# Memory's root applied to the products, wide chunks for the keys' weights, and another order of the first loads

## The chip, the cores and the metric

One Trainium2 chip, one of its cores. The metric is the device time of one launch, in microseconds. Engines are named as in the profile: PE is TensorE (PEld its weight loads), DVE is VectorE, ACT is ScalarE, POOL is GpSimd, SP is SyncE, which here only issues DMAs.

## The reference, cut to what matters

The whole reference is three transformer-like layers on a sequence of 256 tokens of width 2048, with a memory of 256 tokens. What the change touches is how memory's keys and values come about, for the second and the third layer:

```python
def rms_norm_2(x, w):
    xf = x.astype(jnp.float32)
    y = xf * lax.rsqrt(jnp.mean(xf * xf, axis=-1, keepdims=True) + EPS)
    return (y * w.astype(jnp.float32)).astype(x.dtype)

mem_n = rms_norm_2(mem, mem_norm_w)                 # 256 x 2048
k = (mem_n @ w_mk).reshape(b_, -1, MEM_HEADS, MEM_HEAD_DIM)   # 2048 x 512, once per layer
v = (mem_n @ w_mv).reshape(b_, -1, MEM_HEADS, MEM_HEAD_DIM)   # 2048 x 512, once per layer
```

The first layer's input is modulated: silu(c) times w_ada (2048 x 6144) gives shift, scale and gate, and h = rms_norm(x) * (1 + scale) + shift, which is multiplied with w_in.

## The kernel before, in words

Activations are kept transposed: 16 tiles of 128 features by 256 tokens. Every large product is a `Gemm` (line 88), cut into blocks of output columns and chunks of 0.5 MB of weights. For each chunk SP loads the raw weights into one of 7 slots (line 391), ACT writes a rounded high part (`split_hi`, line 410), DVE the remainder as low part (`split_lo`, line 416), and TensorE multiplies (`run_products`, line 457): high weights with the high and low halves of x side by side (line 484, 512 columns), low weights with the high half of x (line 485, 256 columns). For values, kept by token, x is the stationary side and each tile takes six matmuls of 512 columns (lines 478 to 480). A chunk's slot is loaded again once the chunk is used; ACT and DVE split 3 chunks ahead (AHEAD). PSUM holds two sets of two banks for the products (SETS, `set_of`), and a block may start once the block two before it has been taken out.

The order of the work is that of `ORDER` (line 341), the same on all engines. First stand the four products on memory, `G_MEM` (line 291): keys of the second layer (8 chunks of 4 tiles x 256 columns, two blocks side by side), values (8 chunks of 2 tiles x 512 columns), keys and values of the third layer: 32 chunks, called units 0 to 31 here. Behind them come the products on xA, the first layer's normed input.

All other work is hung between the chunks by hooks, written out by hand as positions (i, p) or units. In the memory stage these are: the sum of squares of x on ACT (`norm_square`, line 626), on GpSimd (`add_squares`, line 572, three of four groups are added in pairs) and on TensorE (`sum_squares`, line 1801, matmuls with a matrix of ones from the constants con; line 1810), ending in a root on ACT (`norm_inverse_root`, line 647); and the sums of silu(c) w_ada on DVE (`ada_add`, line 1213), 32 steps in units 0 to 27. GpSimd issues the loads of w_ada (line 588) into a ring of 6 buffers: load m may be issued when the step 6 before it is done. At unit 28 TensorE turns the sums into columns (`modulation_columns`, line 1829), and in units 29 to 31 ACT and DVE norm the first half of x.

Every engine works its queue in order, so a wait holds all that stands behind it. Before the first product on memory the whole of memory's norm is done: SP loads vec, the four quarters of memory, con, then weights (lines 549 to 559); ACT squares the quarters (line 730) and splits three chunks; GpSimd adds; TensorE sums (line 1839); ACT makes the root; DVE multiplies each tile by gain and root (line 1115), ACT writes the high part to xM (line 660), DVE the low part (line 1122). GpSimd issues its first load of w_ada after its adds. Products of keys are taken out by ACT's copy of one half (line 453) and DVE's add of the other (line 1177), values by one copy (line 451).

## Time and profile before

| what | us |
|---|---|
| median of 3 runs | 1816.09 (1813.1 to 1817.1) |
| the profiled execution | 1821.62 |
| its span | 1819.8 |
| TensorE busy in the span | 1767.1 |

The span is what the profiler records on the core; the profiled execution's own time lies 1.8 us above it. All times inside the trace count from the span's start. A busy TensorE is not TensorE at its peak, since ends of matmuls are modelled; where its granted clock is 0.50 each matmul takes twice as long at the same busy share.

### The profile page before, as it was taken

What the parts mean: (1) busy time and instruction counts of PE and PEld (TensorE: products, weight loads), DVE (VectorE), ACT (ScalarE), POOL (GpSimd) and SP (SyncE); (2) the same over time, 40 slices, a digit from 0 to 9 for tenths busy, and PEclk for the clock granted to TensorE, in tenths of its full rate; (3) what the DMA queues carried; (4) which work ended last, traced back from release to release, by engine and by line L of the source; (5) the groups of instructions that cost most, each with busy time, mean ns of one, the idle gap of its engine ahead of it and who ended that gap; (6) DMA issues with size and microseconds to landing.
All of it is one profiled execution on the core that took longest, in us unless ns stands there. A gap on an engine that the chain in (4) does not pass through costs nothing.

```text
span 1819.8 us, 24336 instructions
## 1 busy us (share of the span) xinstructions
PE 1767.1 (97%) x9667; PEld 1501.8 (83%) x9667; DVE 1289.3 (71%) x1631; ACT 897.1 (49%) x1158; POOL 120.0 (7%) x147
## 2 busy tenths in 40 slices
PE   5899999999999999999999999899999999999997
PEld 4688888777888888888888888788888888888886
DVE  6888978785677756888676777965555667677654
ACT  4444443344465445665344556644444445565532
POOL 2411101010010100111000000000000000000000
PEclk9999999999999999999999999999999999999999
DMA  9989969674445566666654555555566565444563
GB/s 319 358 309 336 337 219 322 222 242 134 146 145 171 185 175 187 193 182 179 165 146 141 152 161 171 164 188 184 187 183 173 169 192 149 124 120 127 162 185 105
DMA packets 311889, 350.70 MB, mean 193 GB/s; under 512 B 11248, under 2 KB 286832, under 8 KB 311776
## 3 DMA queue, kind: packets, MB, share of 16 engines
q1 hardware_dynamic: 297792, 298.34, 54.3%
q0 software_dynamic: 13984, 50.80, 7.9%
q8 instruction: 78, 1.28, 0.3%
q14 instruction: 35, 0.29, 0.1%
HBM read 347.00 MB, written 2.10 MB: 192 GB/s over the span
## 4 chain that ended last, share of the span: by engine, by line
PE 78%; DVE 12%; ACT 4%; issue 3%; DMA 2%; POOL 0%; SPq 0%; ACTq 0%; DVEq 0%
PE psG L484 42%; PE psG L485 21%; DVE w_lo L418 4%; PE psG L478 2%; PE psG L479 2%; PE psG L480 2%; ACT w_hi L414 2%; PE psH L1810 1%; DMA raw<-in_mem_w 1%; PE psH L1799 1%; DMA ada_ring<-in_w_ada 1%; DVE P L1177 1%; PE psH L1824 1%; DVE P L1182 1%; PE psH L2108 1%
## 5 line engine op out<-in xcount | busy, mean ns | idle before, releaser
L484 PE MATMUL psG<-xA,w_hi 128*128 128x512 f32 x2624 | 947.0, 404 | 3.4 <-DVE w_lo L418 3.4
L418 DVE TENSOR_TENSOR w_lo<-raw,w_hi 128x1024 fp32r<-128x1024 f32 (+1 forms) x560 | 688.9, 1241 | 262.0 <-ACT w_hi L414 260.6
L485 PE MATMUL psG<-xA,w_lo 128*128 128x256 f32 x2624 | 737.4, 281 | 0.0
L414 ACT ACTIVATE w_hi<-raw 128x1024 fp32r<-128x1024 f32 (+1 forms) x560 | 569.4, 1043 | 233.1 <-PE psG L485 166.3
L484 PEld LDWEIGHTS psG<-xA,w_hi 128*128 128x128 f32 x2624 | 494.6, 188 | 129.0 <-issue 14.9
L485 PEld LDWEIGHTS psG<-xA,w_lo 128*128 128x128 f32 x2624 | 497.7, 190 | 4.1 <-issue 3.6
L484 PE MATMUL psG<-yP,w_hi 128*128 128x512 f32 x960 | 340.0, 398 | 3.1 <-DVE P L1182 1.6
L485 PE MATMUL psG<-yP,w_lo 128*128 128x256 f32 x960 | 269.2, 280 | 0.0
L484 PEld LDWEIGHTS psG<-yP,w_hi 128*128 128x128 f32 x960 | 180.2, 188 | 47.4 <-DVE P L1182 1.9
L453 ACT ACTIVATE P<-psG 128x512 f32<-128x512 f32 (+2 forms) x103 | 61.0, 592 | 247.4 <-PE psG L485 247.4
L485 PEld LDWEIGHTS psG<-yP,w_lo 128*128 128x128 f32 x960 | 181.3, 189 | 0.2
L1177 DVE TENSOR_TENSOR P<-psG,P 128x512 f32<-128x512 f32 (+2 forms) x103 | 70.4, 683 | 115.7 <-ACT P L453 115.7
L1224 DVE SCALAR_TENSOR_TENSOR ada_sum<-ada_ring,silc,ada_sum 128x1024 f32<-128x1024 f32 x60 | 77.9, 1302 | 0.1
L588 POOL DMA_DIRECT2D ada_ring<-in_w_ada x96 | 50.8, 530 | 329.8 <-DVE ada_sum L1224 133.2
L577 POOL TENSOR_TENSOR W<-W 128x512 f32<-128x512 f32 x15 | 25.8, 1720 | 664.3 <-ACT W L632 664.3
L1197 DVE TENSOR_TENSOR xT<-psG,xT 128x512 f32<-128x512 f32 x32 | 22.1, 692 | 54.5 <-PE psG L485 53.9
L484 PE MATMUL psG<-xM,w_hi 128*128 128x512 f32 x128 | 47.6, 413 | 5.3 <-DVE xM L1122 4.8
L478 PE MATMUL psG<-w_hi,xA 128*128 128x512 f32 x128 | 52.7, 411 | 0.0
L484 PE MATMUL psG<-xQ,w_hi 128*128 128x512 f32 x144 | 51.1, 399 | 0.0
L479 PE MATMUL psG<-w_lo,xA 128*128 128x512 f32 x128 | 51.0, 399 | 0.0
L480 PE MATMUL psG<-w_hi,xA 128*128 128x512 f32 x128 | 50.9, 398 | 0.0
L485 PE MATMUL psG<-xQ,w_lo 128*128 128x256 f32 x144 | 40.4, 281 | 0.0
(311 smaller groups left out, 1768.1 us busy)
## 6 DMA issues: line engine op xcount, KB each, us to landing
raw<-in_w_in SPq DMA_DIRECT2D x360, 512.0 KB, 3.8
raw<-in_w_out SPq DMA_DIRECT2D x128, 512.0 KB, 3.5
ada_ring<-in_w_ada POOLq DMA_DIRECT2D x96, 512.0 KB, 6.1
raw<-in_mem_w SPq DMA_DIRECT2D x32, 512.0 KB, 8.8
raw<-in_w_uq SPq DMA_DIRECT2D x24, 384.0 KB, 3.3
raw<-in_w_ukv SPq DMA_DIRECT2D x32, 128.0 KB, 2.4
raw<-in_w_ukv SPq DMA_DIRECT2D x16, 256.0 KB, 3.4
P<-in_memT SPq DMA_DIRECT2D x4, 512.0 KB, 5.8
```

The source lines that it names most:

```text
L414: nc.scalar.activation(high(n), low(n, raw), ACT.Copy).then_inc(hi_ready, 1)
L418: nc.vector.tensor_tensor(low(n), low(n, raw), high(n), ALU.subtract).then_inc(lo_ready, 1)
L453: nc.scalar.activation(g.dst(b), product(g, b, 0), ACT.Copy).then_inc(copied, 1)
L478: nc.tensor.matmul(out, x_hi, hi[:, w], start=first, stop=False)
L479: nc.tensor.matmul(out, x_hi, lo[:, w], start=False, stop=False)
L480: last = nc.tensor.matmul(out, x_lo, hi[:, w], start=False, stop=end)
L484: nc.tensor.matmul(psG[:, bank + f, :], hi[:, w], x, start=first, stop=False)
L485: last = nc.tensor.matmul(psG[:, bank + f, S:2 * S], lo[:, w], x[:, 0:S], start=False, stop=end)
L577: nc.gpsimd.tensor_tensor(a[:, 0:512], a[:, 0:512], a[:, 512:1024], ALU.add).then_inc(q["nm_pair"], 1)
L588: pool.dma_start(ada_ring[slot][:, :], ada_rows(k, part, half)).then_inc(ada_loaded[slot], 16)
L1177: ins = v.tensor_tensor(out, product(g, b, 1), out, ALU.add)
L1224: v.scalar_tensor_tensor(out=out, in0=src, scalar=silc[:, k:k + 1], in1=out, op0=ALU.mult, op1=ALU.add).then_inc(ada_used, 1)
```

## The change

Memory's products are now made on memory times the norm's weights (gain), without the root. The root of each token is applied when the products are taken out: for keys DVE multiplies the block with the root, laid out along tokens, in tile 80 of P (as products of the later layers already do); for values, where tokens are partitions, ACT scales its copies by a column, which TensorE makes from the root by two matmuls of one column. The high parts of memory's tiles are written by ACT from the raw tiles and the low parts by DVE, four tiles at a time: the first four before the products, the others in units 0, 2 and 4. The squares of memory move from before the products into ACT's units 0, 1, 3 and 5, its sums into TensorE's units 3 to 6, its root into unit 7; the squares and sums of x move to units 8 to 14 and 10 to 16.

The keys' weights come as 2 tiles x 512 columns, as the values' do: 8 chunks for both blocks together, which use all four banks and end together. SP's first loads are vec, memory 0, weights 0 and 1, memory 1, weights 2 and 3, memory 2, weights 4, memory 3, weights 5 and 6, con, weights 7, x. GpSimd waits for memory's second quarter and then issues its loads of w_ada; memory's adds stand before its loads 6, 7 and 9, those of x before loads 12, 14 and 17. DVE's w_ada steps lie in units 4 to 28, two in units 4, 8, 12, 16, 20, 24 and 28 and one in the others.

```diff
@@ -99,17 +100,18 @@
...
     def __init__(self, kt, blocks, src, x, dst=None, cols=256, kk=4, ready=None, tokens=None, pair=False, rows=NP,
-                 bias=None, by_tile=False, adds=False, per=None, norm=None):
+                 bias=None, by_tile=False, adds=False, per=None, norm=None, wide=False):
         self.kt, self.blocks, self.src, self.x, self.dst, self.cols, self.kk = kt, blocks, src, x, dst, cols, kk
...
         self.copied, self.by_scalar = not adds and bool(dst), not adds and bool(tokens)
-        self.chunks, self.parts = kt // kk, cols // NP
-        self.order = [(b, c) for b in range(blocks) for c in range(self.chunks)]
+        self.chunks, self.parts, self.wide = kt // kk, cols // NP, wide
+        self.order = [(b, c) for b in range(1 if wide else blocks) for c in range(self.chunks)]
         if pair:
             self.order[0:2 * self.chunks] = [(b, c) for c in range(self.chunks) for b in range(2)]
-        self.last = [self.order.index((b, self.chunks - 1)) for b in range(blocks)]
+        self.last = [self.chunks - 1 if wide else self.order.index((b, self.chunks - 1)) for b in range(blocks)]
+        self.elements = kk * cols * (blocks if wide else 1)
         self.c0 = self.b0 = self.landed0 = self.copied0 = 0
@@ -289,11 +292,16 @@
...
         G_MEM = []
+        def whole_rows(i):
+            return lambda block, chunk: rows(mem_w, (i * KT + 2 * chunk) * NP, 2, 0, 512)
         for i in range(2):
-            at0 = dict(x=lambda k: xM[:, k, :], ready=norm_ready(0))
-            G_MEM += [Gemm(KT, 2, columns(mem_w, 0, row0=2 * i * KT * NP), dst=lambda b, i=i: memkv[:, 8 * i + 2 * b:8 * i + 2 * b + 2, :],
-                           pair=i == 0, **at0),
-                      Gemm(KT, 1, columns(mem_w, 0, 512, 2, row0=(2 * i + 1) * KT * NP), cols=512, kk=2,
+            at0 = dict(x=lambda k: xM[:, k, :], ready=norm_ready(0), kk=2, norm=0)
+            G_MEM += [Gemm(KT, 2, whole_rows(2 * i), dst=lambda b, i=i: memkv[:, 8 * i + 2 * b:8 * i + 2 * b + 2, :],
+                           wide=True, **at0),
+                      Gemm(KT, 1, whole_rows(2 * i + 1), cols=512,
                            tokens=by_head(memkv[:, 8 * i + 4:8 * i + 8, :]), **at0)]
@@ -382,13 +390,13 @@
...
             g = CHUNKS[n][0]
-            return w_hi[:, n % HIGH_SLOTS, 0:g.kk * g.cols]
+            return w_hi[:, n % HIGH_SLOTS, 0:g.elements]
...
             g = CHUNKS[n][0]
-            return (w_lo if t is None else t)[:, PLACE["weight", n] % SLOTS, 0:g.kk * g.cols]
-        def load_weights(sp, g):
+            return (w_lo if t is None else t)[:, PLACE["weight", n] % SLOTS, 0:g.elements]
+        def load_weights(sp, g, behind=None):
             j = PLACE["weight", g.c0]
@@ -402,6 +410,8 @@
...
                     sp.dma_start(out, src).then_inc(raw_loaded[j % SLOTS], 16)
+                if behind:
+                    behind(c)
@@ -428,8 +438,9 @@
...
                 hook(s, p + 1)
-                if i == g.last[b]:
-                    block_done(b)
+                for block in range(g.blocks):
+                    if i == g.last[block]:
+                        block_done(block)
@@ -448,8 +459,12 @@
...
                     src = src.rearrange("p h (t d) -> p h t d", t=4)
+                if g.norm is not None:
+                    nc.scalar.activation(out[:, 0], src[:, 0], ACT.Copy, scale=mem_root_col[:, 0:1])
+                    nc.scalar.activation(out[:, 1], src[:, 1], ACT.Copy, scale=mem_root_col[:, 1:2]).then_inc(scalar_landed, 1)
+                    return
                 nc.scalar.activation(out, src, ACT.Copy).then_inc(scalar_landed, 1)
-            elif g.bias is None or g.norm:
+            elif g.bias is None or g.norm is not None:
                 nc.scalar.activation(g.dst(b), product(g, b, 0), ACT.Copy).then_inc(copied, 1)
@@ -458,9 +473,10 @@
...
                 n, bank = g.c0 + i, set_of(g, b)
-                if c == 0 and g.b0 + b >= SETS:
-                    before, block = BLOCKS[g.b0 + b - SETS]
-                    landed(pe, before, block + 1)
+                for a in range(2 if g.wide else 1):
+                    if c == 0 and g.b0 + b + a >= SETS:
+                        before, block = BLOCKS[g.b0 + b + a - SETS]
+                        landed(pe, before, block + 1)
                 if g.ready:
@@ -479,10 +495,12 @@
...
                     else:
-                        for f in range(g.parts):
-                            w = slice(kk * g.cols + f * NP, kk * g.cols + f * NP + NP)
-                            nc.tensor.matmul(psG[:, bank + f, :], hi[:, w], x, start=first, stop=False)
-                            last = nc.tensor.matmul(psG[:, bank + f, S:2 * S], lo[:, w], x[:, 0:S], start=False, stop=end)
+                        width = g.elements // g.kk
+                        for f in range(width // NP):
+                            w = slice(kk * width + f * NP, kk * width + f * NP + NP)
+                            to = set_of(g, b + f // g.parts) + f % g.parts
+                            nc.tensor.matmul(psG[:, to, :], hi[:, w], x, start=first, stop=False)
+                            last = nc.tensor.matmul(psG[:, to, S:2 * S], lo[:, w], x[:, 0:S], start=False, stop=end)
                     if kk == g.kk - 1:
@@ -513,7 +531,7 @@
...
-            return C("dup", S) if n == 2 else W[:, 1536:1536 + S] if n == 3 else W[:, 0:S]
+            return (P[:, MEM_ROOT, :], W[:, 0:S], C("dup", S), W[:, 1536:1536 + S], W[:, 0:S])[n]
@@ -549,12 +567,21 @@
...
             sp.dma_start(vec[:, :], io["vec"]).then_inc(loaded["vec"], 16)
-            for g in range(4):
+            def load_memory(g):
                 sp.dma_start(mem_raw[:, 4 * g:4 * g + 4, :], io["memT"].rearrange("(t p) s -> p t s", p=NP)[:, 4 * g:4 * g + 4, :])\
                   .then_inc(mem_loaded[g], 16)
-            sp.dma_start(con[:, :], io["con"]).then_inc(loaded["con"], 16)
+            def beside_first(c):
+                if c in (1, 3, 4):
+                    load_memory((1, 3, 4).index(c) + 1)
+                if c == 6:
+                    sp.dma_start(con[:, :], io["con"]).then_inc(loaded["con"], 16)
+            load_memory(0)
             for g in ORDER:
-                load_weights(sp, g)
+                load_weights(sp, g, beside_first if g is G_MEM[0] else None)
                 if g is G_MEM[0]:
@@ -569,20 +596,22 @@
...
         def _(pool):
-            def add_squares(n):
-                for g in range(3):
+            def add_squares(n, groups=range(3)):
+                for g in groups:
                     a = norm_squares(n, g)
...
-            add_squares(0)
+            pool.wait_ge(mem_loaded[1], 16)
             for m, (half, k, part) in enumerate(ADA_ORDER):
                 slot = ADA_SLOT[m]
-                if m == 20:
-                    add_squares(1)
+                if m in (6, 7, 9):
+                    add_squares(0, [(6, 7, 9).index(m)])
+                if m in (12, 14, 17):
+                    add_squares(1, [(12, 14, 17).index(m)])
                 if ADA_BEFORE[m] is not None:
@@ -654,8 +683,8 @@
...
                 for t in tiles:
-                    act.wait_ge(q["nm_h"], 16 * n + t + 1)
-                    x_hi = (hA if n else xM)[:, t, 0:S]
+                    act.wait_ge(q["nm_h"], t + 1)
+                    x_hi = hA[:, t, 0:S]
                     if shift is None:
@@ -725,18 +754,34 @@
...
-            for g in range(4):
+            def mem_hi(g):
                 act.wait_ge(mem_loaded[g], 16)
-                norm_square(0, g, mem_raw)
+                for t in range(4 * g, 4 * g + 4):
+                    f(xM[:, t, 0:S], mem_raw[:, t, :], ACT.Copy, scale=V("mem_norm", t)).then_inc(q["nm_hi"], 1)
+            def mem_root():
+                norm_inverse_root(0)
+                act.wait_ge(q["mem_col"], 1)
+                f(mem_root_col, psH[:, BC, 0:2], ACT.Copy).then_inc(q["mem_col"], 1)
+                act.wait_ge(q["mem_col"], 2)
+            mem_hi(0)
             first()
-            norm_inverse_root(0)
-            norm_hi(0)
             def mem_hook_1(unit):
-                if unit in (6, 8, 11, 13):
+                if unit in (0, 2, 4):
+                    mem_hi(unit // 2 + 1)
+                if unit in (0, 1, 3, 5):
+                    norm_square(0, (0, 1, 3, 5).index(unit), mem_raw)
+                if unit == 7:
+                    mem_root()
+                if unit == 8:
                     act.wait_ge(loaded["x"], 16)
-                    norm_square(1, (6, 8, 11, 13).index(unit), xT)
-                if unit == 18:
+                if unit in (8, 10, 12, 14):
+                    norm_square(1, (8, 10, 12, 14).index(unit), xT)
+                if unit == 19:
                     norm_inverse_root(1)
@@ -1117,18 +1162,12 @@
...
                     dve.wait_ge(q["nm_hi"], 16 * n + u + 1)
-                    x = (xA if n else xM)[:, u, :]
+                    x = xA[:, u, :]
                     if shift is None:
...
                                                in1=x[:, 0:S], op0=ALU.add, op1=ALU.subtract).then_inc(q["nm_lo"], 1)
-            def norm(n, src, gain):
-                dve.wait_ge(q["nm_rs"], n + 1)
-                for t in range(KT + 2):
-                    norm_step(n, src, gain, None, t, 0, KT)
@@ -1175,7 +1214,7 @@
...
                     ins = v.tensor_tensor(out, product(g, b, 1), out, ALU.add)
-                    if g.norm:
+                    if g.norm is not None:
                         link(ins)
@@ -1224,8 +1263,15 @@
...
+            def mem_lo(g):
+                for t in range(4 * g, 4 * g + 4):
+                    dve.wait_ge(q["nm_hi"], t + 1)
+                    v.scalar_tensor_tensor(out=xM[:, t, S:2 * S], in0=mem_raw[:, t, :], scalar=V("mem_norm", t),
+                                           in1=xM[:, t, 0:S], op0=ALU.mult, op1=ALU.subtract).then_inc(q["nm_lo"], 1)
+            mem_lo(0)
             first()
-            norm(0, mem_raw, V("mem_norm", 0, 16))
@@ -1247,7 +1293,10 @@
...
                 for u in range(units):
-                    done.append(done[-1] + (u < units - 4) + (units == MEM_UNITS and u < 4) - (units == EARLY_UNITS and u % 9 == 8))
+                    if units == MEM_UNITS:
+                        done.append(done[-1] + (4 <= u < units - 3) + (4 <= u < units - 3 and u % 4 == 0))
+                    else:
+                        done.append(done[-1] + (u < units - 4) - (u % 9 == 8))
                 return done
@@ -1256,6 +1305,8 @@
...
                         u = u0 + 8 * b + p // 2
+                        if units == MEM_UNITS and u in (0, 2, 4):
+                            mem_lo(u // 2 + 1)
                         for m in range(done[u], done[u + 1]):
@@ -1835,14 +1886,23 @@
...
-            pe.wait_ge(loaded["con"], 16)
-            sum_squares(0)
             def mem_tail_hook(i, p):
-                if (i, p) in ((1, 5), (1, 9), (1, 15), (2, 3)):
-                    sum_squares(1, [((1, 5), (1, 9), (1, 15), (2, 3)).index((i, p))])
-                if 8 * i + p // 2 == MEM_UNITS - 4 and p % 2:
+                u = 8 * i + p // 2
+                if p % 2 == 0:
+                    return
+                if u == 3:
+                    pe.wait_ge(loaded["con"], 16)
+                if u in (3, 4, 5, 6):
+                    sum_squares(0, [u - 3])
+                if u == 7:
+                    pe.wait_ge(q["nm_rs"], 1)
+                    for h in range(2):
+                        ins = mm(psH[:, BC, h:h + 1], norm_root_of(0)[:, h * NP:h * NP + NP], ident[:, 0:1], start=h == 0, stop=h == 1)
+                    ins.then_inc(q["mem_col"], 1)
+                if u in (10, 12, 14, 16):
+                    sum_squares(1, [(10, 12, 14, 16).index(u)])
+                if u == MEM_UNITS - 4:
                     modulation_columns(0)
```


## Rows read from the trace of the kernel before

**Rows 1.** The page: busy time, share and instructions of each engine.

```profile
PE 1767.1 (97%) x9667; PEld 1501.8 (83%) x9667; DVE 1289.3 (71%) x1631; ACT 897.1 (49%) x1158; POOL 120.0 (7%) x147
```

**Rows 2.** Stretches: length; busy us of PE, PEld, DVE, ACT, POOL; clock; DMA; GB/s.

```profile
0.00:25.40 25.40, 6.71 (x15) 4.38 (x15) 8.12 (x18) 11.65 (x17) 9.35 (x16) 0.97 0.97 330
25.40:30.70 5.30, 5.30 (x17) 4.52 (x18) 5.30 (x15) 2.97 (x8) 0.00 (x0) 0.50 0.58 231
...
51.30:54.70 3.40, 0.01 (x1) 0.01 (x1) 3.40 (x5) 1.73 (x3) 0.90 (x2) 0.99 1.04 402
54.70:58.00 3.30, 3.30 (x8) 2.62 (x9) 3.30 (x4) 1.55 (x2) 0.69 (x2) 0.50 1.03 400
...
64.70:67.50 2.80, 0.02 (x1) 0.00 (x0) 2.45 (x2) 0.35 (x2) 2.72 (x3) 1.00 1.03 390
67.50:71.50 4.00, 3.94 (x11) 3.13 (x12) 4.00 (x3) 2.86 (x3) 3.92 (x4) 0.60 1.05 364
...
84.00:108.10 24.10, 24.10 (x138) 21.11 (x137) 19.48 (x17) 10.40 (x12) 3.92 (x8) 1.00 1.01 365
```

**Rows 3.** Timeline of TensorE, 10 to 136 us: start, duration, what; in brackets its wait.

```profile
11.43 2.07 PE L1810 MATMUL psH<-W,con 128*128 128x256 f32 x4 [11.43 <-DMA con<-in_con]
...
54.69 0.79 PE L478 MATMUL psG<-w_hi,xM 128*128 128x512 f32 x1 [3.50 <-DVE memkv L1177]
...
67.56 0.70 PE L1810 MATMUL psH<-W,con 128*128 128x256 f32 x2 [2.84 <-POOL W L579]
...
135.16 0.39 PE L484 MATMUL psG<-xA,w_hi 128*128 128x512 f32 x1
```

**Rows 4.** Timeline of all engines, first 20 us.

```profile
5.34 1.06 ACT L632 ACTIVATE W<-P 128x1024 f32<-128x1024 f32 x1 [1.94 <-DMA P<-in_memT]
...
15.89 3.29 POOL L588 DMA_DIRECT2D ada_ring<-in_w_ada  x6
```

**Rows 5.** Timeline of ScalarE and of VectorE, 50 to 82 us.

```profile
52.70 1.06 ACT L414 ACTIVATE w_hi<-raw 128x1024 fp32r<-128x1024 f32 x1 [1.21 <-DMA raw<-in_mem_w]
...
56.45 1.06 ACT L414 ACTIVATE w_hi<-raw 128x1024 fp32r<-128x1024 f32 x1 [2.21 <-DMA raw<-in_mem_w]
...
68.56 2.25 DVE L418 TENSOR_TENSOR w_lo<-raw,w_hi 128x1024 fp32r<-128x1024 f32 x1
...
72.42 2.31 DVE L418 TENSOR_TENSOR w_lo<-raw,w_hi 128x1024 fp32r<-128x1024 f32 x1
...
78.67 1.21 DVE L418 TENSOR_TENSOR w_lo<-raw,w_hi 128x1024 fp32r<-128x1024 f32 x1
...
81.00 1.21 DVE L418 TENSOR_TENSOR w_lo<-raw,w_hi 128x1024 fp32r<-128x1024 f32 x1
```

**Rows 6.** Landings: SP's chunks 5, 6 (issued 11.6, 13.1), chunk 7 (30.9), xT (31.3); load 6 (36.0).

```profile
DMA to landing us min/median/max: 8.8/10.2/11.5
...
DMA to landing us min/median/max: 4.1/4.1/4.1
...
DMA to landing us min/median/max: 10.0/10.0/10.0
...
DMA to landing us min/median/max: 7.2/7.2/7.2
```

**Rows 7.** Instructions on tile W, 0 to 130 us: ns least, median, most; first and last start.

```profile
L660 ACT ACTIVATE xM<-W x16: 416/417/419, 22.1 to 32.4; 128x256 fp32r<-128x256 f32 x16
...
L577 POOL TENSOR_TENSOR W<-W x6: 1260/1272/2275, 6.5 to 71.4; 128x512 f32<-128x512 f32 x6
L579 POOL TENSOR_TENSOR W<-W x6: 722/1162/1605, 7.8 to 73.7; 128x256 f32<-128x256 f32 x6
```

**Rows 8.** Groups by form, 0 to 140 us: busy us, mean ns, idle before.

```profile
L1177 DVE TENSOR_TENSOR memkv<-psG,memkv 128x512 f32<-128x512 f32 x4 | 2.8, 688 | 2.6 <-ACT memkv L453 2.6
...
L453 ACT ACTIVATE memkv<-psG 128x512 f32<-128x512 f32 x4 | 2.4, 588 | 7.8 <-PE psG L485 7.8
L1221 DVE TENSOR_SCALAR ada_sum<-ada_ring,silc 128x1024 f32<-128x1024 f32 x3 | 2.2, 749 | 0.0
```

More of the change, by code:

```diff
@@ L74 @@
 MEM_UNITS, EARLY_UNITS = 32, 40
+MEM_ROOT = 80
 GATE_RING = 3
@@ L222, in build @@
         ones, ident = C("ones"), C("ident")
+        mem_root_col = col[:, 16:18]
         raw_loaded = [sem(f"raw_loaded{i}") for i in range(SLOTS)]
@@ L236, in build @@
             "rt_t0 rt_rot rt_s rt_qk rt_D rt_z rt_at rt_o rt_os rt_mu rt_xc rt_sq rt_var rt_ln rt_rs rt_y "
-            "f1_yz f1_y f1_hi f1_lo dt_abs dt_ln dt_cum cum_hi cum_lo dt_T dt_col "
+            "f1_yz f1_y f1_hi f1_lo dt_abs dt_ln dt_cum cum_hi cum_lo dt_T mem_col "
             "cv_acc cv_tap cv_a cv_e cv_l cv_b cv_s cv_done xt xd_done "
@@ L626, in norm_square @@
             def norm_square(n, g, src):
-                if n and g == 0:
+                if n > 1 and g == 0:
                     act.wait_ge(q["nm_lo"], 16 * n)
@@ L1443, in dt_hook @@
                     dve.wait_ge(q["dt_T"], 1)
-                    v.tensor_copy(P[:, SCOL, 0:160], psH[:, BA, 0:160]).then_inc(q["dt_col"], 1)
+                    v.tensor_copy(P[:, SCOL, 0:160], psH[:, BA, 0:160])
             def conv_hook(n, p):
```

## The prediction

> **What bounds the kernel now.** I read the page first [rows 1]: TensorE is busy 97% of the span, so only its idle and half-clock time can be won. The touched code runs in the first 135 us. So next came the stretches of that stage [rows 2]: TensorE waits in 0 to 25.4, in 51.3 to 54.7 and in 64.7 to 67.5, and after the first of these gaps the clock is 0.50 (1.2 GHz instead of 2.4) for 5.3 us, after the second 0.50 for 3.3 us, after the third 0.60 for 4.0 us. From 71.5 on TensorE never waits. Memory's products end at 135.16, where the first product on xA starts [rows 3]; what follows is not touched. The change is worth what it moves that 135.16. The same view says what TensorE waited for: con, DVE's add on memkv, GpSimd's adds [rows 3]. The DMA engines are full (share 0.97 to 1.04) through most of 0 to 71.5 [rows 2], so an earlier start of TensorE meets a supply limit.
>
> **The change, part by part.** I work the new schedule forward from the start, with durations of [rows 4 to 8].
>
> *Start of products.* Removed: the wait for the root. Now memory's tiles 0 to 3 need only their own 0.5 MB. It landed at 5.3 [rows 4]. ACT's four tiles of 0.42 us [rows 7] end at 6.95, the first weight split (1.06 [rows 5]) at 8.0, DVE's split (1.21 [rows 5]) at 9.3. TensorE starts at 9.3 instead of 25.4. A chunk of keys' weights is 2.78 us of products at full clock: the second keys' 8 chunks are 24.1 us [rows 2] less the sum's 1.73 us (4 matmuls of 0.43). The first 5.3 us of products were at half clock before [rows 2], so chunk 0 takes 5.1 and ends at 14.4; chunks 1 to 3 end at 22.9. Their tiles and splits are there: SP's transfers of 0.5 MB land 1.5 us apart (con, fifth in the queue, at 11.43 [rows 3], chunk 5, six later, at 11.6 + 8.8 = 20.4 [rows 6]), so at the same places of the queue chunk 2 lands at 11.4, chunk 3 at 12.9.
>
> *The constants are late.* TensorE now asks for con at the end of chunk 3 (for the ones of the sum of squares), and con stands behind 11 transfers of 0.5 MB on SP's queue. In order and undisturbed it lands at 5.3 + 11 x 1.5 = 21.8: the lower bound. But GpSimd issues its six loads of w_ada as soon as memory's second quarter is in, at 9.9. In the trace w_ada's six were issued from 15.9 [rows 4], and chunk 6, which shared with them, took 4.2 us instead of 1.5 (20.4 to 24.6) [rows 6]. Later, chunks that shared with w_ada came 3.75 us apart (ACT waits for them to 52.70 and 56.45 [rows 5]). Twelve transfers of SP and six of GpSimd, 0.52 MB each, and vec's 0.2 are 9.6 MB; at the 330 GB/s of 0 to 25.4 and the 402 of 51.3 on [rows 2] all of it is in by 28.3: the upper bound, if con is last. I take C = 27.8, next to the upper bound, because w_ada's loads are issued 6 us earlier than before. The Trainium skill ("DMA: Bandwidth & Descriptors", Queues, rings and completion order) says that a DMA engine goes round robin between its queues, packet by packet; by that rule alone con would be at the upper bound too, while the trace lets chunks 3 to 5 by undisturbed and slows only chunk 6. So TensorE waits 22.9 to 27.8, as long as the gaps after which the clock fell.
>
> *A chain through four engines at units 3 to 5.* After C: the sum's matmul (0.43 to 0.6), which releases ACT's third square (it waits for the first group's sum): C + 1.7. Then ACT splits chunk 7 (landed C + 1.4): C + 2.75; DVE's split C + 4.0; DVE's last four low tiles (0.42 each) C + 5.7; DVE's first w_ada step (0.75 [rows 8]) C + 6.4. Only now may GpSimd issue load 6 (0.53), and its second pair of adds stands behind that load: 1.26 + 0.72 at the least, as in the start where DVE was quiet, so C + 9.1; 2.27 + 1.60 at the most, beside DVE's work, so C + 10.9 [rows 7]. TensorE wants this sum at the end of chunk 4, C + 0.6 + 2.78 + 2.0 (half clock) = C + 5.4: a second wait of 3.7 to 5.5. Chunk 5 then ends at C + 14.5 to 16.3. The third adds stand behind load 8, which waits for DVE's unit 5, which waits for chunk 8. Chunk 8 lands behind xT, which alone takes 6.3 us (35.0 to 41.3 [rows 6]): C + 8.5. Split, split, DVE step, load, adds: C + 14.8 to 16.6. The fourth sum (1.73), chunks 6 and 7 (5.56) and the two column matmuls end at C + 22.9 to 24.7.
>
> *Keys' products taken out.* Both blocks now end together and each has one more multiplication by the root. ACT's copy of the column 0.3 and of both blocks 0.59 each, DVE's add 0.69 [rows 8] and a multiplication of the same form 0.69 before block 0's banks are free: 2.5 us. Values' products start at C + 25.4 to 27.2; I take 54.2, where before they started at 54.69. So 16 us of head start have shrunk to 0.5.
>
> *From there to the end.* Before: 135.16 - 54.69 = 80.5. Saved: the wait for GpSimd (2.8) and the half clock behind it (4.0 x 0.40 = 1.6), since x's sums now stand at least two units behind their squares. Added: the second keys' products need all four banks, so they wait for ACT's two scaled copies of the values (2 x 0.59 + 0.1 = 1.3), and the second values' products wait for copy, add and multiplication (0.59 + 0.69 + 0.69 and two handovers = 2.3). A clock lost after such a short gap is worth 0 to 1.65 (3.3 x 0.50); half of it, 0.8. Sum 80.5 - 2.8 - 1.6 + 1.3 + 2.3 + 0.8 = 80.5.
>
> *Other edits.* The norm pass on DVE was two operations for each of 16 tiles and becomes one, so DVE gets some 16 x 0.42 back (a tile's time taken as ACT's [rows 7]), in the start, where it waits anyway. It spends 4 x 0.69 on the root. Its w_ada steps move from units 0 to 27 to units 4 to 28 (1.25 a unit): a split and a step take 2.33 (78.67 to 81.00 [rows 5], the step 1.2 of it), with 0.25 x 1.2 more 2.63 us a unit, beside TensorE's 2.72 to 2.78: hidden, with little cover. If it went, unit 28's modulation would wait for the last step, 1 to 2 us. GpSimd's six pairs of adds all run beside DVE now, instead of three: 3 x 1.9 more on GpSimd. Keys' weights come in rows of 2 KB instead of 1 KB. The values' weights already do, and the engines moved 402 GB/s then against 330 in the start [rows 2]: 0.2 us less per chunk at the most, which is inside my C. Same bytes, same count of matmuls.
>
> *Sum.* 54.2 + 80.5 = 134.7 against 135.16: -0.5 us. The profiled execution took 1821.6 in all (span 1819.8), so it would be 1821.1; that execution lies 5.5 above the median of the runs, 1816.1, and I put the change on the median: **1815.6 us**. About 0.2% (3.6 us) is what a measurement can tell from no change.
>
> **The rivals.**
> *Faster: w_ada lets SP go first.* xT was not slowed by loads issued at 36.0 (it landed at 41.3, 6.3 us after chunk 7; the first of them landed at 43.2 [rows 6]). If con lands at 21.8, the first wait is gone and C is set by chunk 3, 22.9. The rest of the chain is the same: values start at 48.3 to 50.1, the change is -5.6 on average: 1810.5. Against it speaks chunk 6's 4.2 us. Were the chain itself shorter by a wait, the gain would be of this size too. No more: with no wait at all values would start at 9.3 + 2.6 + 22.3 + 3.0 + 2.5 = 39.7, a gain of 15.
> *Slower: GpSimd's adds beside DVE.* Both pairs of adds in the chain run at 2.27 + 1.60, and con at its upper bound: values start at 28.3 + 27.2 + 1.9 = 57.4; each gap costs the clock its full 1.65 twice (+2.5 beside my 0.8), and DVE, slowed by x's three groups (a split and a step took 3.86 beside an add, 68.56 to 72.42, instead of 2.33 [rows 5]: 4.6 in all), reaches unit 28 last by 1. Sum +2.7 +2.5 +1 = 6.2: 1822. It decides once the second adds end later than C + 10.9. For it: three of three groups beside DVE were slow. Against it: DVE stands idle before chunk 8 lands, just when the second adds run. The Trainium skill ("SBUF — State Buffer", the shared port pair) says that GpSimd and a DVE operation with two inputs from SBUF lock each other out for a whole instruction. The rows agree: DVE's split took 2.25 there, against 1.21.
>
> **How the numbers follow.** Forecast case, within 3.6 us of no change: 0.46. Faster rival, which also takes the cases in which a wait of the chain is shorter than I put it: 0.32. Slower rival: 0.22. The forecast's own range is 1812.5 to 1819.5; with the rivals' centres most of the way in, 1808.5 to 1821.5.
>
> **What would show it.** Right: first product near 9.3; a TensorE wait for con of about 5 us after chunk 3, one for GpSimd's add of 4 to 5 after chunk 4; half clock behind each; values' first product near 54; no wait for GpSimd in 60 to 75; waits of 1.3 and 2.3 at the two later hand-overs; the first product on xA near 134.7. Wrong: con landed before 23, or values starting before 50, or DVE steps that keep TensorE from unit 28.

## Result, and the profile after

The changed kernel takes 1821.39 us (median of 20 runs, 1813.54 to 1832.26), the kernel before, beside it on the same chip, 1815.41 (20 runs). The ratio is 1.0044, interval 1.0032 to 1.0057: **slower by 0.44%, some 8 us**. I had forecast 1815.6 and "within 0.2%". The range held the time, by 0.1 us, and only because its upper end lay next to the slower rival's 1822; the forecast case was wrong, and so was the direction of its 0.5 us.

The profiled execution took 1832.26 us (span 1830.4), the slowest of its 20 runs; that of before lay some 6 us above its median. So the traces tell where time goes, and the ratio how much. The first view is TensorE's timeline after the change, from answers for several short windows: start, duration, what, and in brackets the wait. It answers to [rows 3].

```profile
9.79 0.76 PE L502 MATMUL psG<-xM,w_hi 128*128 128x512 f32 x1 [9.79 <-DVE w_lo L428]
...
28.73 0.79 PE L1861 MATMUL psH<-W,con 128*128 128x256 f32 x1 [5.47 <-DMA con<-in_con]
...
38.53 0.80 PE L1861 MATMUL psH<-W,con 128*128 128x256 f32 x1 [3.48 <-POOL W L606]
...
44.83 0.48 PE L1861 MATMUL psH<-W,con 128*128 128x256 f32 x1 [1.32 <-POOL W L606]
...
55.53 0.79 PE L494 MATMUL psG<-w_hi,xM 128*128 128x512 f32 x1 [2.34 <-DVE memkv L1221]
...
78.03 0.48 PE L1861 MATMUL psH<-W,con 128*128 128x256 f32 x1 [0.74 <-POOL W L606]
...
82.90 0.47 PE L502 MATMUL psG<-xM,w_hi 128*128 128x512 f32 x1 [1.40 <-issue]
...
110.95 0.79 PE L494 MATMUL psG<-w_hi,xM 128*128 128x512 f32 x1 [3.88 <-DVE memkv L1221]
...
128.40 0.83 PE L1875 MATMUL psH<-con,ada_sum 128*128 128x1 f32 x6 [0.84 <-DVE ada_sum L1263]
...
143.47 0.39 PE L502 MATMUL psG<-xA,w_hi 128*128 128x512 f32 x1
```

Memory's stage ends at 143.47 instead of 135.16: these 8.3 us are as much as the 8 us between the medians (the spans of the two profiled executions differ by 10.6). Until the values' products start only 0.8 us is lost (55.53 against 54.69); 7.5 us are lost behind them, where I had put nothing. Stretches of the trace after, with the columns of [rows 2], show how:

```profile
28.70:35.10 6.40, 6.32 (x18) 4.97 (x18) 5.56 (x11) 4.66 (x8) 0.00 (x0) 0.52 1.10 352
...
55.50:60.00 4.50, 4.47 (x13) 3.57 (x14) 4.47 (x5) 1.85 (x2) 0.56 (x2) 0.64 0.05 17
...
83.00:107.00 24.00, 24.00 (x136) 20.80 (x136) 19.07 (x16) 8.64 (x10) 5.18 (x10) 1.00 1.01 364
107.00:110.90 3.90, 0.07 (x1) 0.00 (x0) 3.72 (x5) 3.24 (x5) 0.53 (x1) 0.88 1.03 393
110.90:116.50 5.60, 5.55 (x13) 4.39 (x14) 5.57 (x6) 0.07 (x1) 0.98 (x2) 0.50 0.50 170
...
128.40:133.40 5.00, 5.00 (x32) 5.00 (x33) 1.23 (x1) 0.70 (x1) 0.53 (x1) 0.71 1.07 373
```

Lost behind the values' start in the changed kernel: waits of 0.74, 1.40, 3.88 and 0.84; half clock after the longest, 5.6 x 0.50 = 2.8; the modulation's columns at a clock of 0.71, 5.0 x 0.29 = 1.5. Together 11.1. Before it was the wait of 2.84 and 4.0 x 0.40 = 1.6, so 4.4 [rows 2, 3]. The difference, 6.7, is most of the 7.5; the rest I didn't itemise.

The chain of waits of the changed kernel up to 145 us (start, duration, what) names what lies under the two late waits:

```profile
96.01 10.03 DMA raw<-in_mem_w
116.47 7.15 DMA raw<-in_mem_w
125.88 2.48 DVE ada_sum L1263 x2
128.40 5.14 PE psH L1875 x32
```

Weights issued at 96.01 land 10 us later. ScalarE and VectorE show what comes of it, in their timelines after the change:

```profile
102.09 1.06 ACT L424 ACTIVATE w_hi<-raw 128x1024 fp32r<-128x1024 f32 x1 [2.95 <-DMA raw<-in_mem_w]
106.06 1.06 ACT L424 ACTIVATE w_hi<-raw 128x1024 fp32r<-128x1024 f32 x1 [2.91 <-DMA raw<-in_mem_w]
...
107.15 1.23 DVE L428 TENSOR_TENSOR w_lo<-raw,w_hi 128x1024 fp32r<-128x1024 f32 x1 [1.54 <-ACT w_hi L424]
108.29 1.28 DVE L1263 SCALAR_TENSOR_TENSOR ada_sum<-ada_ring,silc,ada_sum 128x1024 f32<-128x1024 f32 x1
109.48 0.69 DVE L1216 TENSOR_TENSOR memkv<-psG,memkv 128x512 f32<-128x512 f32 x1
```

Chunks arrive 4.0 us apart where TensorE uses one in 2.7 to 2.8. ScalarE waits for each, VectorE's split is late, and the add that frees the keys' banks, at 109.48, stands behind that split and a w_ada step. The wait is put down to the add on memkv, but its cause is a load.

The reason is in the DMA queues. This is the issues' part of the DMA view for 84 to 105 us (KB each, median us from issue to landing), first before:

```profile
ada_ring<-in_w_ada POOLq DMA_DIRECT2D x7, 512.0 KB, 5.5
raw<-in_mem_w SPq DMA_DIRECT2D x7, 512.0 KB, 5.8
```

and after:

```profile
ada_ring<-in_w_ada POOLq DMA_DIRECT2D x8, 512.0 KB, 7.3
raw<-in_mem_w SPq DMA_DIRECT2D x7, 512.0 KB, 8.3
```

By GpSimd's timelines, 12 loads of w_ada are issued between 34 and 60 us before, and only 6 after; up to 84 us it is 26 against 21. In 55.5 to 60 the DMA engines of the changed kernel stand at a share of 0.05, in 83 to 107 at 1.01. The kernel before has 1.01 in 84 to 108.1 as well, and moves as much there, 365 GB/s against 364 [rows 2]. So the late stretch is full in both; the difference is what had been loaded ahead of it. The kernel before did its w_ada work early, when TensorE was waiting anyway.

### The profile page after: what moved, and what is told of

Read it like the earlier page. It is cut to its first block, busy times and chain, and to the rows that moved or that the text cites. A ratio compares the mean times of both kernels' runs of the same rounds, so it can differ in the third digit from the quotient of the medians.

```text
span 1830.4 us, 24336 instructions
## 1 busy us (share of the span) xinstructions
PE 1775.4 (97%) x9671; PEld 1507.6 (82%) x9671; DVE 1289.4 (70%) x1619; ACT 898.4 (49%) x1161; POOL 122.4 (7%) x147
## 4 chain that ended last, share of the span: by engine, by line
PE 78%; DVE 11%; ACT 4%; issue 3%; DMA 3%; POOL 0%; ACTq 0%; DVEq 0%; SPq 0%
PE psG L502 43%; PE psG L503 21%; DVE w_lo L428 3%; DMA raw<-in_mem_w 2%; PE psG L494 2%; PE psG L495 2%; PE psG L496 2%; ACT w_hi L424 2%; PE psH L1875 1%; PE psH L1850 1%; PE psH L1861 1%; DVE ada_sum L1263 1%; PE psH L2168 1%; PE psH L2169 1%; DVE P L1216 1%
## 5 line engine op out<-in xcount | busy, mean ns | idle before, releaser
L502 PE MATMUL psG<-xM,w_hi 128*128 128x512 f32 x128 | 51.4, 440 | 11.2 <-DVE w_lo L428 9.8
L502 PEld LDWEIGHTS psG<-xM,w_hi 128*128 128x128 f32 x128 | 26.8, 209 | 18.0 <-issue 11.6
```

The lines of the kernel that those rows point to most:

```text
L502: nc.tensor.matmul(psG[:, to, :], hi[:, w], x, start=first, stop=False)
```

## The experiments

Twelve kernels were run, each timed beside the kernel before. xA is the start of the first product on xA in the profiled execution; landing is the median time from issue to landing of the six to eight weight loads issued in 84 to 105 us.

| kernel | ratio | 95% | xA, us | landing, us |
|---|---|---|---|---|
| before | 1 | | 135.16 | 5.8 |
| after | 1.0044 | 1.0032 to 1.0057 | 143.47 | 8.3 |
| e1_con_early | 1.0062 | 1.0037 to 1.0087 | 142.88 | 8.7 |
| e2_adds_first | 0.9998 | 0.9979 to 1.0017 | 138.81 | 9.2 |
| e3_fewer_bytes | 1.0031 | 1.0013 to 1.0049 | 135.95 | 4.1 |
| e4_narrow_second | 1.0034 | 1.0017 to 1.0051 | 141.51 | 7.3 |
| e5_steps_first | 1.0006 | 0.9985 to 1.0026 | 133.50 | 7.3 |
| e6_adds_and_steps | 0.9994 | 0.9972 to 1.0016 | 131.48 | 7.1 |
| e7_and_narrow | 1.0016 | 0.9996 to 1.0035 | 134.71 | 8.5 |
| e8_loads_later | 1.0081 | 1.0050 to 1.0111 | 146.97 | 8.3 |
| e9_adds_steps_8_to_14 | 0.9995 | 0.9980 to 1.0011 | 136.15 | 10.8 |
| e10_steps_of_change | 1.0042 | 1.0025 to 1.0059 | 138.19 | 9.7 |
| e11_steps_and_narrow | 1.0021 | 1.0003 to 1.0040 | 137.79 | 9.7 |
| e12_adds_only | 1.0019 | 1.0004 to 1.0034 | 137.98 | 8.7 |

**The start: con ahead of memory's other quarters.**

```diff
+                if c == 3:
+                    sp.dma_start(con[:, :], io["con"]).then_inc(loaded["con"], 16)
                 if c in (1, 3, 4):
                     load_memory((1, 3, 4).index(c) + 1)
-                if c == 6:
-                    sp.dma_start(con[:, :], io["con"]).then_inc(loaded["con"], 16)
```

> The changed kernel, with con loaded right behind weights 3 instead of behind weights 6. Chain theory: TensorE's wait for con (5.5 us) goes, but the chain through ACT, DVE and GpSimd is then held by the landing of weights 7 and of xT with weights 8 behind it, so TensorE waits longer for GpSimd's adds after chunk 4 and 5; the first product of the values comes at 53 to 55 instead of 55.5, and the time falls by 0 to 2 us. Rival, the constants are what costs: the wait of 5.5 and the half clock behind it (6.3 us at 0.51, so 3 us) both go, values start near 47 to 48, and the time falls by 7 to 8 us.

The wait for con is gone, and TensorE stops elsewhere; the first product on the values comes at 56.85, later than I expected. TensorE's waits of 25 to 150 us in this kernel:

```profile
PE psH L1861 <- POOL W L606: 7.3, 3, 5.2
PE psG L502 <- DVE xM L1270: 7.2, 1, 7.2
PE psG L494 <- DVE memkv L1221: 6.2, 2, 3.9
```

It now waits 7.2 us for xM instead of 5.47 for con. Memory's third quarter isn't what is late: issued at 5.47, it lands 12.1 us later, at 17.6. But ScalarE's copies of it stand behind the split of a chunk of weights that is issued at 9.12 and lands 18.9 us later, at 28.0. The start is bound by what has to come in, not by con.

**The start: memory's adds together, ahead of load 6.**

```diff
-                if m in (6, 7, 9):
-                    add_squares(0, [(6, 7, 9).index(m)])
+                if m == 6:
+                    add_squares(0)
```

> The changed kernel, with all three of memory's pairs of adds on GpSimd ahead of its load 6 of w_ada, so that they no longer stand behind loads that wait for DVE's steps. Chain theory: TensorE's waits for GpSimd of 3.5 and 1.3 us go and with them one stretch of half clock (5 us at 0.68, so 1.6), and the values start at 48 to 50 instead of 55.5. At the end of the stage (first product on xA, 143.5) 4 to 7 us of that are left: the time falls by 4 to 7 us. Rival, the DMA engines bound the whole stage: the values start earlier but later weights are late by as much, and the time falls by less than 2 us.

GpSimd's waits of 3.48 and 1.32 in the start are gone, values start at 48.26 (7.3 earlier, more than the two waits' 4.8), and the ratio falls to 0.9998. So the loads that stand ahead of memory's adds on GpSimd's queue were a real part of the cost. The gain shrinks on the way: values start 7.3 earlier, xA comes only 4.7 earlier, because the weights still land late (9.2 us) and the later waits grow to 4.55 and 1.53.

**The bytes: loads 20 to 31 of w_ada bring 256 of 1024 columns.** This kernel leaves out that part of the modulation's weights.

```diff
-                pool.dma_start(ada_ring[slot][:, :], ada_rows(k, part, half)).then_inc(ada_loaded[slot], 16)
+                w = 256 if 20 <= m < 2 * ADA_HALF // 2 else 1024
+                pool.dma_start(ada_ring[slot][:, 0:w], ada_rows(k, part, half)[:, 0:w]).then_inc(ada_loaded[slot], 16)
```

> The changed kernel, in which w_ada's loads 20 to 31 bring 256 of 1024 columns (the modulation of the first layer's first half of features is computed from stale columns for the rest, so that part of the computation is left out). Bytes theory (two w_ada steps in each fourth unit and one in the others ask for more than the DMA engines give, and weights 24 to 26 and 31 land late): the second values' products wait 2.3 to 2.5 instead of 3.9 us, there is no wait of 0.84 for the last step, and the first product on xA comes at 139 to 141.5 instead of 143.5. Rival, DVE's own work is what is late: the same waits within 0.3 us and the first product on xA within 0.5 us of 143.5.

In the trace it does what the supply theory says, and more than I expected: weights land in 4.1 us, the wait of 3.88 becomes 2.14, that for the last step is gone, xA comes at 135.95. What is left of the first, 2.1, is near the 2.3 of hand-over that I had worked out. But the ratio, 1.0031, can't be told from the change's 1.0044. One profile shows the supply as the cause of the wait; the times neither confirm nor refute it.

**The hand-over: the second keys' weights in chunks of 4 tiles x 256 columns again.**

```diff
+            keys = dict(wide=True, **at0) if i == 0 else dict(at0, kk=4)
-            G_MEM += [Gemm(KT, 2, whole_rows(2 * i), dst=lambda b, i=i: memkv[:, 8 * i + 2 * b:8 * i + 2 * b + 2, :],
-                           wide=True, **at0),
+            G_MEM += [Gemm(KT, 2, columns(mem_w, 0, row0=2 * i * KT * NP) if i else whole_rows(0),
+                           dst=lambda b, i=i: memkv[:, 8 * i + 2 * b:8 * i + 2 * b + 2, :], **keys),
```

> The changed kernel, with the second keys' weights again in chunks of 4 tiles x 256 columns, one block after the other, so that the banks change hands between single blocks. Hand-over theory: the waits of 1.4 us before and 3.9 us behind the second keys' products go, and with the second one the half clock behind it (2.8) and the modulation's columns at half clock (1.5): the first product on xA comes at 134 to 136 instead of 143.5 and the time falls by 7 to 9 us, to that of the kernel before. Rival, the late weights are what counts and the hand-over only shows them: TensorE waits for the low parts of weights inside the second keys' or values' products instead, 2 to 4 us in all, and the time falls by 3 to 5 us.

Both hand-over waits vanish, as expected, but TensorE then waits 3.3 us for the last w_ada step, and xA comes at 141.51, nearer to the rival. The time can't be told from the change's (1.0034). The hand-overs were not what bounded this stretch; behind them stood the steps.

**The steps: two per unit in units 4 to 10, one in 11 to 28.** In the change a second step comes in every fourth unit.

```diff
-                        done.append(done[-1] + (4 <= u < units - 3) + (4 <= u < units - 3 and u % 4 == 0))
+                        done.append(done[-1] + (4 <= u < units - 3) + (4 <= u < 11))
```

> The changed kernel, with the seven units of two w_ada steps at 4 to 10 instead of at 4, 8, ... 28 (one step in each of 11 to 28). Bytes theory: the DMA engines carry the extra loads while TensorE waits in the first keys' products anyway, weights 24 to 26 and 31 land in time; the second values wait 2.1 to 2.5 us instead of 3.9, TensorE doesn't wait for the last step, and the first product on xA comes at 137 to 140 instead of 143.5; the time falls by 3 to 6 us. Rival, it is the sum of the bytes that is too large, wherever the steps stand: other weights are late instead and the first product on xA comes at 142 to 145.

TensorE's waits from 25 to 135 us in this kernel:

```profile
PE psH L1861 <- POOL W L606: 6.5, 2, 5.0
PE psH L1861 <- DMA con<-in_con: 5.4, 1, 5.4
PE psG L494 <- DVE memkv L1221: 4.5, 2, 2.3
PE psG L502 <- issue: 1.4, 1, 1.4
```

The start is as in the change (values at 55.38), the wait at the second hand-over is 2.14, there is none for a step, and the modulation's columns take 3.63 us instead of 5.14. xA comes at 133.50, 10 us earlier, and the ratio is 1.0006, its interval below the change's. **Moving only the w_ada steps takes the change's loss back.** So did the adds' edit of e2, so this is one of two repairs. This kernel, too, leaves the DMA engines at a share of 0.05 in 55.4 to 60, so the idle stretch is not the cost by itself: here 11 loads are issued in 60 to 84 us (9 in the change), and in 84 to 105 us the engines move 398 GB/s against 364.

**Combinations.** Adds and steps together:

> The changed kernel, with both: GpSimd's three pairs of memory's adds ahead of load 6, and two w_ada steps in units 4 to 10, one in 11 to 28. If the two losses are separate, they add up: the values start at 48 to 50, the first product on xA comes at 131 to 135, and the time is 0.1 to 0.5% below the kernel before. If both draw on the same limit of the DMA engines, the first product on xA stays at 136 to 139 and the time within 0.15% of the kernel before.

The earliest xA of all, 131.48, as expected if the losses are separate, but the time is not: 0.9994 isn't told from the kernel before. Both cures draw on the same VectorE time: at unit 7's double steps it is behind, and the first hand-over's wait grows to 6.3. With the narrow second keys as well:

> As the one before, and the second keys' weights in chunks of 4 tiles x 256 columns again. With the weights in time the hand-over is worth what it costs by itself: the waits of 1.4 and 2.1 to 2.3 us go and most of the half clock behind the second (1.5 to 2.8), so the first product on xA comes 4 to 6 us earlier than in the kernel before this one of the same call, and the time is 0.3 to 0.8% below the kernel before. Rival, the weights come late again once TensorE waits nowhere: a wait for a split or a w_ada step of 2 to 4 us takes their place and less than 2 us are won.

1.0016, no gain: a wait of 2.9 for a w_ada step comes back. Without waits at the second keys' hand-overs VectorE has hardly any time left; the windows view of this kernel, 50 to 117 us, has it busy 61.57 of 67.00. The DMA share in the same row is 0.98, so the row doesn't tell which of the two is the limit:

```profile
50.00:117.00 67.00, 62.51 (x299) 52.46 (x300) 61.57 (x54) 26.99 (x30) 21.48 (x31) 0.96 0.98 352
```

The second steps moved to units 8 to 14, adds first:

```diff
-                        done.append(done[-1] + (4 <= u < units - 3) + (4 <= u < units - 3 and u % 4 == 0))
+                        done.append(done[-1] + (4 <= u < units - 3) + (8 <= u < 15))
```

> As the kernel with both edits (GpSimd's adds ahead of load 6, and the pairs of w_ada steps early), but the seven units with two steps are 8 to 14 instead of 4 to 10. In that kernel DVE was still at the steps of unit 7 when TensorE had the first keys' products done, and the values waited 6.3 us (start 51.6). Theory: now they start at 48 to 49, but DVE, which splits and steps without a pause from there on, is the limit at unit 28, so the first product on xA comes at 129.5 to 132 against 131.5, and the time is within 0.15% of that kernel. Rival, TensorE keeps the 3 us: first product on xA at 128 to 129.

0.9995 with xA at 136.15: values start at 48.09, as expected, but the second hand-over waits 6.06, so xA misses the expected 129.5 to 132. The limit I had named, VectorE at unit 28, isn't the one that shows: weights land 10.8 us after issue, and in 84 to 105 us ScalarE waits for them six times, 10.9 us in all. The steps' place can be traded, and the time is the same as before within what can be told. Steps first and narrow keys, without the adds' edit:

> The changed kernel with two w_ada steps in units 4 to 10 and one in 11 to 28, and the second keys' weights in chunks of 4 tiles x 256 columns. The step kernel had its first product on xA at 133.5, with waits of 1.4 and 2.1 us at the two hand-overs and no half clock behind them. Theory: these 3.5 us go as waits, but DVE was only 1 to 2 us ahead there, so it is next: a wait for the last step of 0 to 3 us before the modulation's columns, and the first product on xA at 131 to 134. Rival, the whole 3.5 us are won: 129.5 to 130.5.

1.0021, with 3.5 us of wait for a step, and xA at 137.79 instead of the expected 131 to 134.

**Loads of w_ada only behind memory's last quarter.**

```diff
-            pool.wait_ge(mem_loaded[1], 16)
+            pool.wait_ge(mem_loaded[3], 16)
```

> The changed kernel, with GpSimd's first loads of w_ada behind memory's last quarter instead of its second. Theory: con then lands before 25 and weights 7 by about 28, TensorE's wait for con falls from 5.5 to under 2 us, but DVE's unit 4 (which the second pair of adds waits for) comes only 1 to 3 us earlier, so the values start at 52 to 54.5 instead of 55.5 and the time falls by 1 to 3 us. Rival, the six loads are then late for DVE's first steps: the chain gets longer by as much, the values start at 55 to 57 and the time stays or rises.

The slowest of all, 1.0081. The wait for con is gone, but w_ada is not what comes late, as the rival had it. GpSimd's first six loads now go out from 16.8 us on, together with xT, and the chunk of weights issued behind xT at 17.64 lands 23.0 us later, at 40.66 (issued at 17.74, it lands at 37.45 in the change). ScalarE waits 13.4 us for it, VectorE's split behind it 11.9, GpSimd's adds stand behind VectorE's step, and TensorE waits 10.9 us for them; xA comes at 146.97. Later loads are worse even in the start.

**The kernel before, with the change's steps.** Its x's adds were moved to load 14 too: load 20 waits for step 14, which these steps reach only in unit 14 or 15.

```diff
-                if m == 20:
+                if m == 14:
                     add_squares(1)
...
-                    done.append(done[-1] + (u < units - 4) + (units == MEM_UNITS and u < 4) - (units == EARLY_UNITS and u % 9 == 8))
+                    if units == MEM_UNITS:
+                        done.append(done[-1] + (4 <= u < units - 3) + (4 <= u < units - 3 and u % 4 == 0))
+                    else:
+                        done.append(done[-1] + (u < units - 4) - (u % 9 == 8))
```

> The kernel before, with the w_ada steps at the units of the change (4 to 28, two in each fourth) and x's adds on GpSimd ahead of load 14 instead of load 20 (they would else wait for steps that now come later). Theory of the steps: the adds' wait of 2.8 us and the half clock behind it (1.6) may go, but weights from 20 on land late; TensorE waits 0 to 2 us for them and 1 to 3 us for the last step before the modulation's columns, some of which then run at half clock; the first product on xA comes at 135 to 139 instead of 135.2, the time 0 to 0.2% above the kernel before. Rival, the steps cost only together with keys' blocks that end together: no new wait, the first product on xA at 130.5 to 132, and 0.1 to 0.25% below.

TensorE's waits, 25 to 135 us:

```profile
PE psH L1827 <- DVE ada_sum L1224: 4.4, 1, 4.4
PE psH L1813 <- POOL W L579: 3.5, 1, 3.5
```

and the stretch behind the first of them, with the columns of [rows 2]:

```profile
120.30:127.20 6.90, 6.86 (x33) 6.87 (x33) 1.12 (x1) 0.00 (x0) 0.53 (x1) 0.50 0.93 344
```

With nothing of the change but its steps, and x's adds at load 14, the kernel before becomes 0.42% slower, as much as by the whole change and more than the 0 to 0.2% that I expected. Its xA is only 3.0 us later than before, though, which would be 0.17%; the rest of the 0.42% shows in no stretch that I read. Values start early here, at 50.02, with no steps on VectorE in units 0 to 3, but weights land in 9.7 us, the last step comes 4.38 late, and the modulation runs at half clock for 6.9 us.

**Its control: only the adds moved, the steps as before** (the first hunk above alone).

> The control for the run before it: the kernel before, with x's last two groups of adds ahead of load 14 instead of load 20 and nothing else changed; the steps stay as they were. If the loss of the steps' run was the steps' schedule, this one has its first product on tile xA at 131 to 135.5 us as the kernel before (135.16), no wait of over 1.5 us for an adaptive step ahead of the modulation's columns, and a ratio within 0.998 to 1.001. If it was the adds' place (they then run beside the first keys' products), the first product on xA comes at 137 to 139 us and the ratio is 1.003 to 1.005 again.

A miss. There is no wait for a step, as expected, but xA comes at 137.98 and the ratio is 1.0019, between the two cases that I had named. VectorE's timeline of this kernel:

```profile
50.27 2.29 DVE L1224 SCALAR_TENSOR_TENSOR ada_sum<-ada_ring,silc,ada_sum 128x1024 f32<-128x1024 f32 x1
52.48 1.74 DVE L418 TENSOR_TENSOR w_lo<-raw,w_hi 128x1024 fp32r<-128x1024 f32 x1
...
75.46 1.28 DVE L1224 SCALAR_TENSOR_TENSOR ada_sum<-ada_ring,silc,ada_sum 128x1024 f32<-128x1024 f32 x1 [9.73 <-DMA ada_ring<-in_w_ada]
```

With steps as early as before's, adds at load 14 are early too: from 47.2 on GpSimd stops three times for squares that ScalarE has not made, and issues no load until 70.4 (in 34 to 60 us only 8 loads of w_ada instead of 12). TensorE waits 5.39 us for VectorE ahead of the values, VectorE runs dry for 9.73 us, and TensorE waits 2.3 more. So the control removed the late steps by another way of delaying the loads, and lost too; it can't say how much of e10's 0.42% is the adds' place, and the two intervals overlap. What is common to change, e10 and e12 is that fewer w_ada loads are issued in 34 to 60 us (6, 8 and 8 against 12) and that weights land in 8.3 to 9.7 us at 84 to 105 us instead of 5.8. The loads of that stretch alone don't decide: e5 has 8 there too, but 11 in 60 to 84 (the change 9). Counted up to 84 us, the kernels with 19 to 21 loads (e8, e1, the change, e3, e4) have ratios of 1.0031 to 1.0081, those with 23 to 26 have 0.9994 to 1.0021, but for e10 with 23 and 1.0042.

No kernel is shown to be faster than the kernel before.

## Why the prediction was right or wrong

**Right, up to the values.** The first product came at 9.79 (9.3 expected). Chunks 0 to 3 took 13.5 us (13.6). Con landed just before 28.73 (27.8; the upper bound of 28.3, 28.4 when worked out again, was missed by 0.3 to 0.4). The wait for GpSimd after chunk 4 was 3.48, with 1.32 more after chunk 5 (3.7 to 5.5 for the first). Half clock followed the wait for con (0.52 for 6.4 us). Values started at 55.53 (54.2): one term, con, was 0.9 late, and the chain behind it added 26.8 (25.4 to 27.2). So 16 us of head start did shrink to nothing. The hand-over to the second keys cost 1.40 (1.3).

**Wrong.** The step that failed is the cost of the moved w_ada steps, in *Other edits*: "a split and a step take 2.33 ..., with 0.25 x 1.2 more 2.63 us a unit, beside TensorE's 2.72 to 2.78: hidden, with little cover. If it went, unit 28's modulation would wait for the last step, 1 to 2 us." I costed the moved steps as VectorE's time alone. Each step also triggers a load, 1.25 instead of 1 per unit, and the loads were moved with it from 34 to 60 us, where TensorE waits, to 60 to 125, where it doesn't. By the rows: 0.524 MB of weights and 1.25 x 0.524 of w_ada per unit of 2.75 us is 0.43 MB/us, above the 0.402 of [rows 2]. I had both numbers and didn't divide. Priced, it is 0.43 - 0.40 = 0.03 MB/us, over 24 units of 2.75 us 1.8 MB too much, or some 4.5 us at that rate, less what the slots buffer. Even that is too kind. In the stretch where the weights are late both kernels move only 0.364 to 0.365 MB/us with full DMA engines, less than the 0.38 that one step a unit asks for. What the traces do show to differ is the stock of loads: 26 issued by 84 us before, 21 in the change. Five loads are 2.6 MB, by my estimate 7.2 us at 0.364 MB/us; no run isolates this. Measured over the terms of my sum: 1.6 at the hand-over (3.88 instead of 2.3), 2.0 for its clock (2.8 instead of 0.8), 0.8 for the last step, 1.5 at the modulation, 0.7 for x's third adds: 6.6 of the 7.4 us by which 80.5 was too small. e5, which moves only the steps, gives 10 us of xA and 0.38% back; that the order of the steps costs this much is shown, that it does so through the supply of weights rests on the traces.

Also off: "x's sums now stand at least two units behind their squares" was to end all waits for GpSimd there. The third adds took 2.64 and 1.58 us beside VectorE and were 0.74 late.

**The rivals.** The slower one came out in time (1822 against 1821.39) but not in mechanism. Its deciding point was second adds ending later than C + 10.9; with C at 28.7 they ended at 38.5, C + 9.8, run at the quiet price of 1.27 and 0.73. Its part "reaches unit 28 last by 1" did come (0.84), though from late weights, not from slow adds. e2 shows that taking the adds' chain away is worth about as much as putting the steps right, so either repair brings the kernel back to before. The faster rival needed con at 21.8, and fell: con wasn't in until just before 28.73. The last line of *What would show it*, "DVE steps that keep TensorE from unit 28", was the sign that showed.

**Open.** The share of 0.44% between the late supply and VectorE's own load isn't settled, since e3 moved xA and not the time. Nor does the median landing rank the kernels: it is 10.8 and 9.2 us in e9 and e2, whose times are those of the kernel before. Over all fourteen kernels a later xA goes with a higher ratio, but with exceptions of 0.2 to 0.3% (e2, e3, e10), and the span behind xA differs from profile to profile by up to 14 us (1672.7 in e6, 1686.9 in the change) though its code is the same. Not tried: the kernel after with more than 7 weight slots.

## What to carry to other kernels

When a schedule of side work is shifted, divide bytes by time for each stretch it is moved into, per unit, as one does for each engine, take the rate that the trace shows in that stretch, and count what has been loaded ahead of it; work done while the main engine waits costs little, beside an engine at full speed the same work is not free. A head start at the front is worth only what the first late shared input lets through. A wait that the trace puts on the last link (here an add on memkv) has to be followed back to the load that was late three links before it.

## What the runs showed of the hardware that I had not expected

**The clock after gaps of equal length.** After 3.88 us (the change) and 3.50 us (before) of idle TensorE the granted clock fell to 0.50. After 3.01 us in e6 it stayed at 1.00. After 2.14 us it fell in e3 and stayed in e5. The windows view of e3, then of e5, behind those gaps:

```profile
108.60:113.00 4.40, 4.33 (x12) 3.43 (x13) 4.37 (x6) 0.94 (x1) 0.43 (x1) 0.61 0.22 83
```

```profile
107.90:112.00 4.10, 4.03 (x18) 3.33 (x19) 4.07 (x6) 1.86 (x2) 0.13 (x1) 1.00 0.83 323
```

**A granted clock of 1.00 that isn't speed.** In the first stretch of products after the change the row says 1.00, but 15 matmuls took 4.7 us, as at half clock (17 in 5.3 in [rows 2], its clock 0.50), and the first lasted 0.76 us instead of 0.40:

```profile
9.80:14.50 4.70, 4.70 (x15) 4.02 (x16) 2.93 (x3) 2.87 (x5) 3.29 (x6) 1.00 1.07 373
```

**Who gives way.** In 84 to 105 us of the change w_ada's queue moved 4.54 MB and SP's 3.09, though the weights are what TensorE waits for. These are the queues' rows for that stretch (packets, MB, share of the packets' time):

```profile
q0 software_dynamic: 1251, 4.54, 59.0%
q1 hardware_dynamic: 1597, 3.09, 40.8%
```

A packet of w_ada's queue carries 3.6 KB on the mean (4.54 MB / 1251), one of SP's 1.9 KB. The Trainium skill ("DMA: Bandwidth & Descriptors", Queues, rings and completion order) says that a DMA engine goes round robin between its queues, packet by packet. The trace agrees in that neither queue starves. It is tempting to put GpSimd's larger share down to its larger packets, but the runs speak against it. The kernels with narrow second keys have smaller packets on SP's queue in the same 84 to 105 us, and SP moves more there, not less: 3.94 MB in e5 (1.9 KB a packet), 4.53 in e11 (1.5 KB); 4.03 in e6, 4.84 in e7; 3.09 in the change, 3.38 in e4. w_ada's queue moves less in each pair: 4.39 and 3.62 MB, 4.21 and 3.26, 4.54 and 3.70. What sets the shares stays open.
